# Six more pairs of blocks as seven quarter products, in a hybrid mixer trunk on one Trainium2 core

## The chip, the cores and the metric

The kernel runs as one program on one core of a Trainium2 chip. The time is the device time of one execution in microseconds. Engines are named as in the profile: PE is TensorE, PEld its weight loads, DVE VectorE, ACT ScalarE, POOL GpSimd, SP the sync engine, which issues most DMAs.

## What is computed

The reference is a decoder trunk of one layer: three token mixers side by side, a merge with gates, and a mixture of experts. 512 tokens and 16 meta tokens, width 1024, float32.

```python
u = _rmsnorm(h, norm_mix[layer]) * valid
(a_q, a_f, a_i, a_g, b_qkv, b_beta, b_decay, b_g,
 c_q, c_k, c_v, c_gk, c_g, gate_logits) = jnp.split(u @ w_in[layer], split_points, axis=-1)
y_a = _hgrn2(a_q, a_f, a_i, a_g, ...)                # 4 heads; q = silu(q_in) / sqrt(dk); output * silu(g_in)
y_b = _gated_deltanet(b_qkv, b_beta, b_decay, b_g, ...)   # 4 heads
y_c = _gla(c_q, c_k, c_v, c_gk, c_g, ...)            # 4 heads; output * silu(g_in)
gates = sigmoid(gate_logits)                          # 3 x 1024 columns
merged = sum(gates * (ys @ w_branch))
h = h + merged @ w_out
h = h + _hier_moe(_rmsnorm(h), ...)                   # top 1 of 4 groups, top 2 of 8 experts
```

Everything that this case is about is in `u @ w_in`: blocks of 128 output channels by 512 tokens (528 where the meta tokens are wanted), with 1024 inputs.

## The kernel before

**Stages.** The setup norms and turns the tokens into uT. Then come the first mixer "a" (HGRN2, four heads r = 0 to 3), the second "b" (gated DeltaNet, four heads), the third "c" (GLA, two halves of two heads), the merge, and the experts. "Channel mixer" in the title words of the change is c.

**Blocks and steps.** `blocks` is one list of all blocks of the input projection in the order in which PE computes them and SP loads their weights (512 KB each, into a ring of six). PE interleaves it with the mixers' own products: `fill(n, last)` computes the next n steps of the list (none past block `last`), `through(stage, seg, r)` all steps up to that block. PE's order is thus fixed by hand, and so are those of DVE and ACT, with semaphores counted by name (`Order`). A block of 512 tokens has 8 steps (L822, one product of 512 columns each), a block of 528 ("wide") 8 steps of two products of 264 (L819, L820). Each float32 product is two instructions in the trace.

**Gate pairs.** Two neighbouring blocks of the merge gates ("t0", "t1", and in stage b also "c" t0 to t3) are computed as a pair of seven quarter products, Winograd's form: 14 steps of two products of 256 columns (`pair_step`, L789), 28 products in place of 32 halves. In order P2, P1, P5, P6, P3, P7, P4. It takes four mixes of weights (S1, S2, S4, S3: 128x512 each, on POOL for stage a in `mix_weights`, L672 to L677, on DVE for b and c), four mixes of tokens once (T1 to T4, 128x1024, on POOL), a copy of P1 on ACT (`keep_product`, before P6), and five sums on DVE (`gate_second`: U2, which P7 waits for; `gate_upper`: U3 and upper; `gate_lower`: corner and lower).

**A head of the first mixer.** Blocks f (wide), q, g, v (wide), t0, t1. PE: `a_out(r-1)` (L907, L908, waits for the last pick of head r-1), fill(4), `a_sum(r-1)` (a sum of squares with ones, L901), through g; then `gd` (diagonal Gram product, L848, waits for k and q), fill(3); seven levels l = 0 to 6, each with a Gram product `gr` (it waits for DVE's zb of that level), small products (turn of keys at 0, of values at 2, states at 4) and a fill of 3 steps (2 at levels 5 and 6); then through the next head's f (in head 3, through b's k). DVE per level: d, za, zb, and a pick P (L1467) of the Gram product before. At a head's start ACT and DVE work from f: softplus, log decay, scan b, `a_finish(r-1)` (y1, y: the normed output of the head before), last differences, d0, then q, qe, ke.

**From the first to the second mixer.** After `a_out(3)`, head 0 of b goes fill(3), `a_sum(3)`, through b's q, fill(6), the key's sum of squares `ssk` (L901, four instructions), through v, fill(4), KK (L875), through g, the turn of b_u (`N`, L869), the turn of the keys, and fills of 4. The bank of b's v waits for the convolution of k (`k3`), the bank of b's g for that of q (`q3`). DVE here goes: last pick of head 3 (L1467), gate sums and gate part of the pair (L1564 to L1572), convolution of k (L1696, L1699), `a_finish(3)`, silu and features of k, convolution of q (L1696, L1699), decays, kn, kb, ..., U (b_u, which N waits for).

**The third mixer.** Blocks k, q, g0, g1, v0, v1, then the merge's blocks. PE: fill(4), sum, through q, fill(3), Gram, fill(5), levels with fill(8). DVE copies g0 and g1 out of PSUM at levels 0 and 1.

Of the kernel before, what the change touches and what calls it, by code (L numbers as in the profile page):

```python
# [11 lines left out]
P = 128  # L12
# [92 lines left out]
def hybrid_trunk(nc, x, meta_tokens, norm_mix, w_in, hgrn_lb_logits, hgrn_norm, gdn_conv, gdn_a_log,  # L105
# [4 lines left out]
    with ctx:  # L110
# [272 lines left out]
        A_SEGS = ["f", "q", "g", "v", "t0", "t1"]  # L383
# [3 lines left out]
        blocks = [("a", s, r) for r in range(A_R) for s in A_SEGS]  # L387
# [9 lines left out]
        PAIRS = len(gate_pairs)  # L397

        def pair_no(stage, r):
            return gate_pairs.index((stage, r))  # L400

        def pair_row(stage, r):

            return {"a": 0, "b": KD, "c": 2 * KD}[stage] + 2 * r

        def pair_block(stage, r):

            return where["c", f"t{2 * (r % 2)}", r // 2] if stage == "c" else where[stage, "t0", r]
# [4 lines left out]
        R_AT = {"a": 0, "b": 2, "c": 0}  # L413
        N_AT = {"a": 2, "b": 1, "c": 2}

        def running(stage):

            return bank(R_AT[stage])[:, 0:TH]

        def upper_parts(stage):  # L420

            return ps[:, R_AT[stage] * 512 + TH:R_AT[stage] * 512 + 3 * TH]

        def lower_parts(stage):

            return bank(N_AT[stage])

        def gate_rows(stage, r):
            return gates[:, pair_row(stage, r):pair_row(stage, r) + 2, :]
# [5 lines left out]
        def block_columns(stage, seg, r):  # L435

            if seg[0] == "t":
# [7 lines left out]
        AT = {"a": {"f": wide(0), "q": real(1), "g": real(0), "v": wide(1)},  # L445
              "b": {"k": wide(0), "q": wide(1), "v": wide(0), "g": real(1)},
              "c": {"k": wide(0), "q": real(0), "g0": real(1), "g1": real(0), "v0": wide(1), "v1": wide(0)}}
# [21 lines left out]
        def each(r, names):  # L469
# [8 lines left out]
                                                                               "kv", "gr5", "gr6"])] + each(A_R - 1, ["o", "ss"]))  # L478
        a_act = Order("a_act", [x for r in range(A_R) for x in
                                each(r, ["ab", "e", "l"]) + each(r - 1, ["oo"] if r else []) + each(r, ["ad", "e2", "l2", "k"]) +  # L480
                                each(r - 1, ["ln", "ri"] if r else []) +
                                each(r, ["eb", "dec", "abq", "eq", "lq", "eke", "sq", "xa0", "xb0", "abg", "eg", "lg", "xa1", "xb1",
                                         "sg", "keTm", "keTr", "xa2", "xb2", "vc", "xa3", "xb3", "v", "vm", "xa4", "xb4",
                                         "xa5", "xb5", "xa6", "xb6"])] + each(A_R - 1, ["oo", "ln", "ri"]))
        a_dve = Order("a_dve", [x for r in range(A_R) for x in
                                each(r, ["ls", "dif", "mx", "tk", "lf", "b"]) + each(r - 1, ["y1", "y"] if r else []) +
                                each(r, ["dbm", "dbr", "d0", "tq", "q", "qe", "ke", "d1", "za0", "zb0", "tg", "Pd", "d2", "za1", "zb1",
                                         "g", "P0", "d3", "za2", "zb2", "P1", "d4", "za3", "zb3", "P2", "d5", "za4", "zb4", "P3",
                                         "d6", "za5", "zb5", "S0", "S1", "S2", "S3", "P4", "za6", "zb6", "P5", "P6"])] +
# [40 lines left out]
        def c_finish_names():  # L530
# [8 lines left out]
                                       {0: ["gc_0"], 1: ["gc_1"], 2: ["tg_0"], 3: ["tg_1", "g_0"], 4: ["g_1"], 5: ["S0", "S1", "S2", "S3"]}.get(l, []))] + both([f"P{LEVELS - 1}"]))] +  # L539
                      each(C_R - 1, c_finish_names()))  # L540

        pair_mix = Order("pair_weights", [f"{n}.{p}" for p in range(A_R) for n in ("S1", "S2", "S4", "S3")])
        delta_mix = Order("delta_weights", [f"{n}.{p}" for p in range(A_R, PAIRS) for n in ("S1", "S2", "S4", "S3")])

        def mixed(name, p):
            return (pair_mix if p < A_R else delta_mix).after(f"{name}.{p}")
        pair_pe = Order("pair_products", [f"{n}.{p}" for p in range(PAIRS) for n in ("P1", "P5", "P6", "P3")])
        pair_copy = Order("pair_copies", [f"{n}.{p}" for p in range(PAIRS) for n in ("P1",)])
# [7 lines left out]
        w = Area(WORK)  # L556
        a_fb, a_k, a_b, a_lf, a_tmp, a_eke = (w.take(TOK) for _ in range(6))
        a_q, a_eb, a_qe = (w.take(SEQ) for _ in range(3))
        a_g = w.take(SEQ)
        a_db = w.take(TOK)  # L560
        a_sg = w.take(SEQ)
        a_dd = [w.take(SEQ) for _ in range(2)]
# [2265 lines left out]
```

## Time and profile before

| | us |
|---|---|
| median of 3 runs | 1070.38 |
| runs | 1070.01, 1070.38, 1071.59 |
| profiled execution, its own time | 1071.85 |
| its span, first to last instruction | 1070.0 |
| PE busy | 1027.7 (96%) |
| DVE busy | 533.1 (50%) |
| ACT busy | 309.8 (29%) |
| POOL busy | 93.0 (9%) |

Mean granted clock of PE 0.986. Stage a runs from 17 to about 225 us, b to about 530, c and the merge to about 730, the rest is output product, router and experts. A span's engines overlap, so the shares don't add up; idle time of an engine costs only where PE, or at the end a DMA, has to wait for it. In the timelines, an instruction's duration includes the time in which it overlaps the next of its engine: the cost of one in a run is the distance from start to start.

### The profile page before, as it was taken

The numbers are of one execution on the slowest core, as the hardware profiler recorded it, in microseconds if no ns is written. First come the engines' busy times: TensorE is split into PE (matmuls) and PEld (weight loads), VectorE is DVE, ScalarE is ACT, GpSimd is POOL, SyncE is SP. The second block draws the span as 40 slices with busy tenths as digits, with TensorE's granted clock in tenths as the row PEclk, the third lists the DMA queues.
The fourth block names the chain that finished last, engine by engine and source line by source line (L and its number), as shares of the span: only waits on it lengthen the run. The fifth ranks groups of instructions, "written<-read, shape, count | busy, mean of one in ns | idle before, by whom it ended". The sixth has DMA issues, their size and how long they took to land. (4 is left out here: it accounts for less than half of the span.)

```text
span 1070.0 us, 20467 instructions
## 1 busy us (share of the span) xinstructions
PE 1027.7 (96%) x8841; PEld 696.1 (65%) x8841; DVE 533.1 (50%) x1058; ACT 309.8 (29%) x573; POOL 93.0 (9%) x89
## 2 busy tenths in 40 slices
PE   9999999999999999999999999999998999877897
PEld 8676766787777877878756656544456665545454
DVE  5766566658468477387454365331344322211114
ACT  3545445334243343344332032010110111101013
POOL 4320202000000000000000000000001222112110
PEclk9999999999999999999999999999998999989899
DMA  9222222142332132141222221174947999999986
GB/s 266 66 70 59 60 61 71 49 83 61 80 76 69 41 84 61 42 92 52 59 61 60 59 60 61 40 274 130 386 147 268 415 413 414 416 415 415 417 327 246
DMA packets 111965, 174.73 MB, mean 163 GB/s; under 512 B 9011, under 2 KB 87100, under 8 KB 103554
## 3 DMA queue, kind: packets, MB, share of 16 engines
q1 hardware_dynamic: 99010, 134.93, 36.5%
q10 hardware_dynamic: 7136, 27.33, 6.4%
q0 software_dynamic: 5728, 11.14, 3.9%
q8 instruction: 71, 1.16, 0.4%
q14 instruction: 20, 0.16, 0.0%
HBM read 169.16 MB, written 12.60 MB: 170 GB/s over the span
## 5 line engine op out<-in xcount | busy, mean ns | idle before, releaser
L789 PE MATMUL ps<-arena 128*128 128x256 f32 x672 | 165.0, 388 | 0.0
L789 PEld LDWEIGHTS ps<-arena 128*128 128x128 f32 x672 | 121.2, 190 | 16.4
L822 PE MATMUL ps<-arena 128*128 128x512 f32 x288 | 128.2, 595 | 1.2 <-DVE arena L1831 1.2
L819 PE MATMUL ps<-arena 128*128 128x264 f32 x400 | 123.1, 389 | 0.8 <-DVE gates L1580 0.8
L820 PE MATMUL ps<-arena 128*128 128x264 f32 x400 | 121.7, 386 | 0.0
L2316 PE MATMUL ps<-arena,gates 128*64 128x256 f32 (+1 forms) x1088 | 106.2, 353 | 16.1 <-DMA arena<-in_expert_w_up 15.8
L1463 DVE TENSOR_TENSOR arena<-arena 128x256 f32<-128x256 f32 (+6 forms) x198 | 95.9, 527 | 48.6 <-ACT arena L1259 36.9
L2316 PEld LDWEIGHTS ps<-arena,gates 128*64 128x64 f32 x1088 | 73.6, 145 | 55.7 <-DMA arena<-in_expert_w_up 25.9
L822 PEld LDWEIGHTS ps<-arena 128*128 128x128 f32 x288 | 53.6, 190 | 62.3 <-issue 61.8
L813 PE MATMUL ps<-yT,arena 128*128 128x512 f32 x192 | 84.8, 596 | 2.1 <-DVE gates L1580 1.4
L820 PEld LDWEIGHTS ps<-arena 128*128 128x128 f32 x400 | 76.0, 190 | 13.0
L819 PEld LDWEIGHTS ps<-arena 128*128 128x128 f32 x400 | 72.5, 190 | 13.2 <-issue 2.8
L2495 DVE COPY gates<-ps 128x1024 f32<-128x1024 f32 x15 | 18.4, 1225 | 101.2 <-PE ps L2297 101.1
L813 PEld LDWEIGHTS ps<-yT,arena 128*128 128x128 f32 x192 | 35.7, 190 | 45.0 <-issue 44.6
L1996 PE MATMUL ps<-arena,gates 128*128 128x512 f32 x128 | 55.8, 592 | 0.0
L2252 POOL DMA_INDIRECT gates<-normed_tokens,gates x16 | 16.6, 1036 | 419.4 <-DVE gates L2087 348.5
L2404 ACT ACTIVATE gates<-ps 128x128 f32<-128x128 f32 x32 | 8.9, 278 | 143.9 <-PE ps L2316 143.9
L1996 PEld LDWEIGHTS ps<-arena,gates 128*128 128x128 f32 x128 | 24.0, 190 | 28.7 <-issue 28.2
L2258 POOL DMA_INDIRECT expert_results<-gates x32 | 32.0, 999 | 121.3 <-ACT gates L2410 118.8
L2325 PE MATMUL ps<-arena,gates 128*64 128x512 f32 x176 | 42.3, 604 | 0.0
L2500 DVE TENSOR_TENSOR gates<-gates,ps 128x128 f32<-128x128 f32 x32 | 9.1, 284 | 61.9 <-ACT gates L2404 61.8
L1467 DVE COPY_PREDICATED arena<-C,ps 128x512 f32<-128x512 int32 x56 | 39.8, 724 | 0.0
(374 smaller groups left out, 1372.2 us busy)
## 6 DMA issues: line engine op xcount, KB each, us to landing
arena<-in_w_in SPq DMA_DIRECT2D x68, 512.0 KB, 3.9
arena<-in_expert_w_gate SPq DMA_DIRECT2D x27, 1024.0 KB
arena<-in_expert_w_up SPq DMA_DIRECT2D x27, 1024.0 KB
arena<-in_expert_w_down ACTq DMA_DIRECT2D x16, 1024.0 KB, 33.1
arena<-in_w_branch SPq DMA_DIRECT2D x12, 512.0 KB, 3.9
arena<-in_expert_w_down SPq DMA_DIRECT2D x6, 1024.0 KB, 27.4
C<-in_expert_w_gate SPq DMA_DIRECT2D x5, 1024.0 KB
gates<-in_expert_w_up SPq DMA_DIRECT2D x5, 1024.0 KB
```

The source lines that it names most:

```text
L789: mm = t.matmul(dst, wt[:, k, :], rhs[:, k, :], start=(k == 0), stop=(k == KH - 1))
L813: mm = t.matmul(merge_bank[b], wt, rhs, start=first, stop=last)
L819: t.matmul(dst[:, 0:HALF], wt, uT[:, k, 0:HALF], start=(k == 0), stop=(k == KD - 1))
L820: mm = t.matmul(dst[:, HALF:], wt, uT[:, k, HALF:], start=(k == 0), stop=(k == KD - 1))
L822: mm = t.matmul(dst, wt, uT[:, k, META:], start=(k == 0), stop=(k == KD - 1))
L1463: v.tensor_tensor(out_, a_, b2, op).then_inc(*q.did(name))
L1467: v.copy_predicated(tiles(pm), over(up(l).bitcast(I32), NT), tiles(src)).then_inc(*q.did(name))
L1996: mm = t.matmul(bank(n), gates[:, k, i * P:(i + 1) * P], wo[:, k, n % 2 * 512:(n % 2 + 1) * 512], start=(k == 0), stop=(k == KD - 1))
L2258: return g.indirect_dma_start(out=y_dram, out_offset=bass.IndirectOffsetOnAxis(ap=which, axis=0), in_=rows, in_offset=None, bounds_check=4 ...
L2316: mm = t.matmul(dst, toks[:, k, :], src, start=(k == 0), stop=(k == KD - 1))
L2325: mm = t.matmul(bank(6 + b)[half * SLOTS:(half + 1) * SLOTS, :], hT[b][:, j * SLOTS:(j + 1) * SLOTS], weights[n][1][:, at:at + 512], start ...
L2495: v.tensor_copy(xT[q % 2], ps[:, 0:2 * 512].rearrange("p (k t) -> p k t", k=KD)).then_inc(pair_read.sem, 1)
```

## The change

The query and output gate blocks of each head of a (q, g), and the two output gate blocks of each half of c (g0, g1), become pairs as the gate pairs are: pairs "qg" (running products in PSUM bank 2, lower ones in bank 7 for head 0; banks 0 and 2 for the others) and "g". 18 pairs instead of 12, by `pairs`. Their results go to a_ql and a_gl (two buffers), or c_g, in SBUF. For this:

- The order of blocks in a becomes f, q, g of head 0, then for each head t0, t1, v, and q, g, f of the next head.
- PE goes through t1 before gd, and fills four steps a level (three at level 0), capped at the next head's f, in head 3 at b's q.
- POOL mixes the weights of ten pairs (qg, a and g) instead of four; the token mixes move to DVE, ahead of its first step of the mixers.
- DVE gets five sums for each new pair: a pair's second and upper sums now sit ahead of the levels, its lower ones at level 0, those of the next head's qg at levels 4, 5 and 6. The query of head r+1 is finished (`a_query`: tq, q on DVE, softplus and exponential on ACT) at the end of head r. `gate_end(r)` on ACT moves from head r+1 into head r, behind it.
- In c, two copies on DVE go, the sums of the new pair come at levels 0 and 1, and the fill at level 0 is 6 instead of 8.

The b loop of PE, DVE and ACT isn't changed.

```diff
-        A_SEGS = ["f", "q", "g", "v", "t0", "t1"]
-        blocks = [("a", s, r) for r in range(A_R) for s in A_SEGS]
+        blocks = [("a", s, 0) for s in ("f", "q", "g")]
+        for r in range(A_R):
+            blocks += [("a", s, r) for s in ("t0", "t1", "v")] + [("a", s, r + 1) for s in ("q", "g", "f") if r + 1 < A_R]
...
+        pairs = [("qg", 0)]
+        for r in range(A_R):
+            pairs += [("a", r)] + [("qg", r + 1)] * (r + 1 < A_R)
+        pairs += gate_pairs[A_R:] + [("g", r) for r in range(C_R)]
...
+        def running_bank(stage, r):
+            return {"qg": 0 if r else 2, "a": 2, "b": 2, "c": 0, "g": 2}[stage]
+
+        def lower_bank(stage, r):
+            return {"qg": 2 if r else 7, "a": 0, "b": 1, "c": 2, "g": 0}[stage]
...
             for r in range(A_R - 1):
-                mix_weights(r)
+                mix_weights("qg", r)
+                mix_weights("a", r)
+            mix_weights("qg", A_R - 1)
             g.wait_ge(*dve0.after("gbrow"))
...
+            for r in range(C_R):
+                mix_weights("g", r)
...
             def wait_for_bank(stage, seg, r):
                 if stage == "a":
                     if seg == "f":
+                        pair_upper_free(pair_no("qg", r))
+                    else:
+                        pair_upper_free(pair_no("a", r))
+                elif stage == "b":
+                    if seg == "k":
                         if r:
+                            pair_upper_free(pair_no("c", r - 1))
                         else:
+                            t.wait_ge(*pair_sum.after(f"lower.{pair_no('a', A_R - 1)}"))
                     elif seg == "q":
+                        t.wait_ge(*(pair_sum.after(f"lower.{pair_no('c', r - 1)}") if r else a_act.after(f"vc.{A_R - 1}")))
                     else:
                         t.wait_ge(*b_dve.after(f"{ {'v': 'k3', 'g': 'q3'}[seg]}.{r}"))
...
-            through("a", "q", 0)
+            through("a", "g", 0)
             small_turned()
             for r in range(A_R):
                 if r:
                     a_out(r - 1)
                     fill(4)
                     a_sum(r - 1)
-                through("a", "g", r)
+                through("a", "t1", r)
...
-                    fill(3 if l < 5 else 2)
+                    fill(4 if l else 3, where["a", "f", r + 1] if r + 1 < A_R else where["b", "q", 0])
                 through(*(("a", "f", r + 1) if r + 1 < A_R else ("b", "k", 0)))
...
                     block_grams(c_zz[l % 2], l, r)
-                    fill(8)
+                    fill(8 if l else 6)
...
+            mix_tokens()
             v.wait_ge(sem("consts_loaded"), 16)
...
                 if r:
                     a_finish(r - 1)
+                    second_sum("a", r)
+                else:
+                    second_sum("qg", 0)
                 v.wait_ge(*a_dve.after(f"b.{r}"))
                 last_diffs(a_dve, a_db, a_b, r)
                 diff(a_dve, a_act, a_dd, a_b, 0, r)
...
                 tt(a_dve, f"ke.{r}", a_eke[:, 0:TOK - P], a_eke[:, 0:TOK - P], a_k[:, 0:TOK - P])
+                if r == 0:
+                    second_sum("a", 0)
+                upper_sums("a", r)
...
-                gate_lower("a", r)
                 gate_part("a", r)
+                if r + 1 < A_R:
+                    v.wait_ge(*a_dve.after(f"zb{LEVELS - 1}.{r}"))
+                    a_query(r + 1)
...
+                    if l == 1:
+                        upper_sums("g", r)
                     if l:
                         for s in range(CH):
...
                             pick(c_dve, f"P{l - 1}_{s}.{r}", c_pm[s], l - 1, gram_bank(s))
-                    if l in (0, 1):
-                        v.wait_ge(*block_done("c", f"g{l}", r))
-                        v.tensor_copy(c_g[l], real(1 - l)).then_inc(*c_dve.did(f"gc_{l}.{r}"))
+                    if l == 0:
+                        second_sum("g", r)
+                    if l == 1:
+                        lower_sums("g", r)
```

## Rows read from the trace of the kernel before

**Rows 1.** page of the profile, section 1, busy us of each engine

```profile
PE 1027.7 (96%) x8841; PEld 696.1 (65%) x8841; DVE 533.1 (50%) x1058; ACT 309.8 (29%) x573; POOL 93.0 (9%) x89
```

**Rows 2.** windows: us, busy us of each engine, granted clock, DMA share, GB/s

```profile
77.00:127.00 50.00, 50.00 (x409) 35.85 (x409) 29.82 (x64) 23.87 (x48) 5.28 (x4) 1.00 0.24 64
226.00:252.00 26.00, 26.00 (x115) 19.09 (x114) 19.93 (x31) 12.60 (x19) 1.77 (x2) 1.00 0.43 86
```

**Rows 3.** timeline of TensorE: start us, us, engine, line, operation, tiles, count

```profile
75.14 0.38 PE L907 MATMUL ps<-arena 128*128 128x128 f32 x2
...
81.22 10.46 PE L822 MATMUL ps<-arena 128*128 128x512 f32 x24
91.52 0.29 PE L969 MATMUL ps<-bcol,C 128*128 128x20 f32 x2
...
251.89 3.62 PE L789 MATMUL ps<-arena 128*128 128x256 f32 x16
255.35 0.83 PE L837 MATMUL ps<-arena 128*128 128x128 f32 x6
```

**Rows 4.** page of the profile, section 5, two groups: busy us, mean ns

```profile
L789 PE MATMUL ps<-arena 128*128 128x256 f32 x672 | 165.0, 388 | 0.0
...
L822 PE MATMUL ps<-arena 128*128 128x512 f32 x288 | 128.2, 595 | 1.2 <-DVE arena L1831 1.2
```

**Rows 5.** timeline of the weight loads, head 3 of the first mixer

```profile
205.70 2.46 PEld L789 LDWEIGHTS ps<-arena 128*128 128x128 f32 x12
```

**Rows 6.** timeline of TensorE, head 3 to the second mixer

```profile
191.61 0.46 PE L848 MATMUL ps<-arena 128*32 128x32 f32 x32
...
215.29 0.68 PE L857 MATMUL ps<-arena 128*64 128x64 f32 x8
...
224.85 0.38 PE L907 MATMUL ps<-arena 128*128 128x128 f32 x2
...
226.63 0.61 PE L819 MATMUL ps<-arena 128*128 128x264 f32 x2
...
230.16 0.61 PE L819 MATMUL ps<-arena 128*128 128x264 f32 x2
...
239.96 1.24 PE L901 MATMUL ps<-arena,ones 128*128 128x512 f32 x4
...
250.80 1.25 PE L869 MATMUL ps<-C,arena 128*128 128x128 f32 x10
```

**Rows 7.** timeline of VectorE, the same stretch

```profile
216.53 0.73 DVE L1467 COPY_PREDICATED arena<-C,ps 128x512 f32<-128x512 int32 x1
...
222.35 1.23 DVE L1572 SCALAR_TENSOR_TENSOR gates<-gates,yT 128x1024 f32<-128x1024 f32 x1 [3.40 <-ACT yT L1205]
225.05 0.77 DVE L1696 TENSOR_SCALAR arena<-ps,rowsT 128x528 f32<-128x528 f32 x1 [1.47 <-PE ps L820]
225.85 2.36 DVE L1699 SCALAR_TENSOR_TENSOR arena<-ps,rowsT,arena 128x527 f32<-128x527 f32 x3
...
232.54 0.69 DVE L1463 TENSOR_TENSOR yT<-arena 128x512 f32<-128x512 f32 x1
...
238.37 2.37 DVE L1699 SCALAR_TENSOR_TENSOR arena<-ps,rowsT,arena 128x527 f32<-128x527 f32 x3
...
248.61 0.82 DVE L1463 TENSOR_TENSOR arena<-ps,arena 128x640 f32<-128x640 f32 x1
```

**Rows 8.** windows around an idle stretch in the experts

```profile
810.00:813.40 3.40, 0.12 (x2) 0.04 (x1) 0.00 (x0) 0.00 (x0) 0.00 (x0) 0.82 0.85 339
813.40:819.00 5.60, 5.51 (x42) 5.14 (x44) 3.46 (x7) 0.00 (x0) 0.99 (x1) 0.50 0.15 37
```

**Rows 9.** timeline of VectorE at the start, beside GpSimd

```profile
21.71 2.22 DVE L302 TENSOR_SCALAR lbc<-lbc 128x4 f32<-128x4 f32 x1
```

**Rows 10.** timeline of GpSimd at the start

```profile
21.54 2.36 POOL L659 TENSOR_TENSOR arena<-arena 128x1024 f32<-128x1024 f32 x1
```

**Rows 11.** timeline of VectorE in head 1, last differences

```profile
84.20 1.24 DVE L1463 TENSOR_TENSOR arena<-arena 128x16 f32<-128x16 f32 x3
```

More of the change, by code:

```diff
@@ new lines, in running, with upper_parts, lower_parts, pair_rows @@
+        def running(stage, r):
+            return bank(running_bank(stage, r))[:, 0:TH]
+        def upper_parts(stage, r):
+            at = running_bank(stage, r) * 512 + TH
+            return ps[:, at:at + 2 * TH]
+        def lower_parts(stage, r):
+            return bank(lower_bank(stage, r))
+        def gate_rows(stage, r):
+            row = {"a": 0, "b": KD, "c": 2 * KD}[stage] + 2 * r
+            return gates[:, row:row + 2, :]
+        def pair_rows(stage, r):
+            if stage == "qg":
+                return a_ql, a_gl[r % 2]
+            if stage == "g":
+                return c_g
+            rows = gate_rows(stage, r)
+            return rows[:, 0, :], rows[:, 1, :]
@@ L558, in hybrid_trunk @@
         a_q, a_eb, a_qe = (w.take(SEQ) for _ in range(3))
-        a_g = w.take(SEQ)
+        a_ql = w.take(SEQ)
+        a_gl = [w.take(SEQ) for _ in range(2)]
         a_db = w.take(TOK)
@@ L758, in pair_step @@
                         t.wait_ge(sem(f"block_loaded{n % RING}"), (n // RING + 1) * 16)
+                        if stage == "g":
+                            t.wait_ge(*c_dve.after(f"f.{r}"))
+                        elif stage == "a":
+                            t.wait_ge(*pair_sum.after(f"{'lower' if r else 'upper'}.{p - 1}"))
+                        elif stage == "qg" and r:
+                            t.wait_ge(*pair_sum.after(f"lower.{p - 1}"))
                     if name == "P5":
@@ L1423, in gate_parts @@
                 def gate_parts(s):
[L1424 removed]
+                    a.wait_ge(*pair_sum.after(f"lower.{pair_no('g', r)}"))
                     softplus(c_act, (f"abg_{s}", f"eg_{s}", f"lg_{s}"), r, c_sg[s], c_g[s])
@@ L1568, in gate_part @@
+                v.tensor_tensor(tiles(row, 2), tiles(lower_parts(stage, r), 2), over(row[:, TH:], 2), ALU.add).then_inc(*pair_sum.did(f"lower.{p}"))
             def gate_part(stage, r):
-                p, rows = pair_no(stage, r), gate_rows(stage, r)
+                p, rows = gate_no(stage, r), gate_rows(stage, r)
                 v.wait_ge(*pair_soft.after(f"soft.{p}"))
```

303 lines of the change are left out of this document (164 added, 139 removed).

## The prediction

> **What bounds the kernel now.** I read the page's busy times first. TensorE is busy 96% of the span, VectorE 50%, ScalarE 29%, GpSimd 9% [rows 1]. Then I read the windows of the mixer stages: in the stretches quoted, TensorE is busy for every microsecond, at the full clock (granted 1.00, so 2.4 GHz), while VectorE has 20 us free of 50 in the first mixer and 6 of 26 at the start of the second [rows 2]. So the time of the mixers is the sum of TensorE's instructions. A product removed is time gained, and a microsecond in which TensorE finds nothing ready is a microsecond lost: no later slack takes it back, since the weights of the experts are loaded only when the mixers are done.
>
> **What the seven products save.** Six pairs of blocks change form (four of the first mixer, two of the channel mixer). One of the blocks costs 8 products of 512 columns, recorded as 16 instructions. In an unbroken run of 24 of them the next start comes 10.30 us later, 0.429 us each, so two blocks are 32 x 0.429 = 13.7 us. The new form is 28 products of 256 columns, 56 instructions; 16 of them take 3.46 us to the next start, 0.216 each, so 12.1 us [rows 3]. Saved: 1.63 us a pair, 9.8 us for six. The bound from below is the page's groups: 165.0 us for 672 instructions at L789 is 13.75 us a pair, and 128.2 for 288 at L822 is 14.24, which leaves 0.5 us a pair, 2.9 in all [rows 4]. That mean is not taken: it holds the breaks where other work comes in between, and the number of breaks stays. So 9.8, or 2.9 at worst.
>
> A rule that speaks against this part is a page's. Twelve weight loads of the pair form last 2.46 us in all, less than 12 x 0.216 = 2.59 us of products beside them [rows 3, 5], so the loads lie beside the products. The Trainium skill, TensorE: Matmul & The Clock Gate, section The mechanism, says that a weight load overlaps products in flight only when it goes to another group of rows. If that held here, each load would stand in the row, and the trace disagrees.
>
> **What moves, and what it uncovers: the handover from the first to the second mixer.** This is the largest term. Before, the steps of head 3 that lie between its first Gram product (gd, L848) and the output (a_out) are: v (8 steps), the gate pair (14 steps), b's k (8 steps). Now the gate pair stands before gd, in all heads. In heads 0 to 2 its place in the levels is taken by the next head's query pair and f block. In head 3 there is no next head: the fills are 3, 3, 4, 4, 4, 4, 4, 4 steps, capped at b's q block, and only v, k, q = 24 steps exist. So 2 remain after Gram 5 and none after Gram 6. From gd of head 3 to the turn of b_u (L869) TensorE needed 250.80 - 191.61 = 59.2 us, all busy [rows 6]. It now has one pair less to do there, 12.1 us. The question is whether VectorE and ScalarE can be that much earlier. I follow their chain. Let X be the end of the last pick of head 3, before 217.25 [rows 7].
> 1. Gram 6 ends about 215.97, the pick at 217.25: 1.3 us with nothing to fill, where two steps and the k block were.
> 2. a_out takes 1.8 us (224.85 to 226.63), so it ends at X+1.9. The next fill(3) is now v, whose bank waits for b's k convolution. VectorE is in order: gate part 1.23, convolution 3.16 (225.05 to 228.21): X+4.4. Idle 2.5.
> 3. Three v steps (2.7) and the sum of squares (0.85) end at X+7.95. The normed y of head 3 ends 3.07 us after that product, as before (230.16 to 233.23): X+11.0. TensorE does the five other v steps up to X+12.4.
> 4. fill(6) used to be six v steps. Five are left, so the sixth is the first step of b's output gate, whose bank waits for b's q convolution. That ends 7.5 us after y (240.74 to 233.23), and its order on VectorE is the same: X+18.5. Idle 6.1. The key's sum of squares (L901 x4) stands behind this step in TensorE's queue and waits with it, though its own input is long there.
> 5. Gate step 0.86 and sum of squares (L901 x4) 1.24, end at X+20.6. b_u ends 8.2 us after the latter (241.20 to 249.43): X+28.85. TensorE's work in between is 7.1 us. Idle 1.3.
> Sum 1.3 + 2.5 + 6.1 + 1.3 = 11.2 us [rows 6, 7]. A second way: 24 wide steps and the small products take 29.6 us from gd to X (before 25.6, with 20 steps of which 12 are short, and two after), and 29.0 from X gives 58.6 for 47.1 us of work, 11.5 idle. Bounds 9 to 13.
>
> **The clock.** An idle stretch of 3.3 us is followed by 5.6 us at a granted clock of 0.50, which is 1.2 GHz [rows 8]. The 6.1 us idle of step 4 is longer. Behind it stand a gate step and the sum of squares, on the chain: some 1.9 us of work that takes 3.8. The 2.5 us idle may do it too, with up to 1.7. I take 2.3, bounds 0 and 5. VectorE then runs up to 1.3 us closer to TensorE than before in the rest of b's head 0 (before, b_u was ready 1.4 us early): knock-on waits 0.8, bounds 0 and 1.5.
>
> **Heads 1 and 2: GpSimd beside VectorE.** GpSimd mixes 10 pairs instead of 4; the four token mixes go to VectorE. One of them has 1024 columns, as the gate part has, 1.23 us [rows 7], so 4.9 us for four; the small setup steps around them are stretched no more by GpSimd's mixes of 2.36, and TensorE has f, the small columns and two products to do before the first product that needs them. Hidden, 0 to 1 us. While GpSimd reads SBUF a VectorE operation with SBUF inputs waits: one of 4 elements took 2.22 us beside GpSimd's 2.36 [rows 9, 10]. [...] The mixes for the next query pair come due right after the gate pair's third, fourth and fifth product, which is when VectorE runs y, the last differences, qe and ke of heads 1 and 2. From the end of f (75.14) VectorE has done the differences at 10.3 us [rows 3, 11]. Prices go by the number of columns: 1.23 us for 1024 and 0.69 for 512 [rows 7], so about 0.4 for 256. The chain now starts some 0.7 us later (ScalarE has the query's exponential and the gate's last one, a step of 1024, ahead of it), and gains 0.4 for the second sum, 1.2 for qe and ke, 1.1 for the two upper sums: 13.7. TensorE wants the bank for v at 1.8 + 12.1 + 0.85 + 0.4 = 15.2. Three GpSimd operations of 1.27 us in between would make 17.5, 2.3 late; one or none makes no wait. I take 1.5 a head for two heads, 3.0, bounds 0 and 5. Head 3 has no mix at that place.
>
> **The channel mixer.** For each half VectorE loses two copies and gains five sums. At level 1 the upper sums wait for the sixth product of the pair, and the two picks of level 0 queue behind them on VectorE: 1.1 + 2 x 0.8 = 2.7 us from that product's end, where TensorE has only the seventh product and the key turn left before Gram 1, 1.73 + 0.4. So Gram 1 waits 0.6 us in each half, 1.2, bounds 0 and 2.5 (none before, when nothing stood ahead of the picks). GpSimd's mixes for the first of them fall into the end of the second mixer: 0 to 1, taken as 0 since VectorE reads PSUM there.
>
> Otherwise the five new sums of a pair (3 x 0.4 + 2 x 0.69 = 2.6 us) and ScalarE's copy are hidden: VectorE is busy 29.8 us of the 50 of a head [rows 2], and a fill is now four steps, 3.46 us, where it was three. Without that cover they would cost 4 x 2.6 = 10 us.
>
> **Sum.** -9.8 + 11.2 + 2.3 + 0.8 + 3.0 + 1.2 = +8.7 us. The profiled execution took 1071.85 us (span 1070.0 and 1.85 around it), 1.5 above the median of 1070.38, and just over the slowest run shown; the difference applies to either. From the median: 1079.1; from the profiled one 1080.6.
>
> **The rivals.**
> - Faster: the handover is covered after all. Its mechanism: the chain from gd of head 3 to b_u is paced by TensorE alone, and shortens with it by 12 us. It decides at the wait of b's first gate step for the q convolution: if that is under 2 us, the saving wins. Then 1070.4 - 9.8 + 1 to 3 = 1060.6 to 1064, say 1062. For it speaks that VectorE has 6 us of 26 free in that stretch [rows 2]; against it that the steps of the chain wait for each other, not for TensorE. Chance 0.11.
> - Nothing to be seen: the handover costs as reckoned, without clock, GpSimd and channel terms, or about half of all: -9.8 + 9 to 11: 1070 to 1072. Chance 0.10.
> - Slower by more: the saving is the page's mean (2.9), or each GpSimd mix blocks VectorE in the levels as well: +15.6 or more, 1086 to 1090. Chance 0.07.
> - Weight loads stand in the row with the products. One lasts 0.205 us [rows 5]. A pair would then pay 24 loads more, 4.9 us, less the 1.6: +3.3 a pair, +19.8 us for six in place of -9.8, so 1079.1 + 29.6 = 1108.7. The rows show the loads beside the products in this very form. The Trainium skill's page on TensorE, named above, is where this rule stands. Chance 0.01.
>
> **How the numbers follow.** The forecast, slower through the handover, 1073 to 1086, has 0.71. Range 1066 to 1087: the lower end leaves out the faster rival, the upper one most of the two slower ones. About 0.2% (2.1 us) is what a measurement here can tell from no change. Faster by more than that 0.11 (the first rival), within it 0.10 (the second), slower 0.79 (the rest).
>
> **What would show it.** Right: in the waits of TensorE a new row of about 6 us for the first b gate step (L822's successor) on VectorE's convolution, one of 2.5 us for b's v block on the same line, a granted clock below 1 in that window alone of the mixers; heads of the first mixer 1.6 us shorter each, but for what GpSimd costs in heads 1 and 2 (a wait of v for the upper sums); 0.6 us at the channel mixer's Gram 1. Wrong: no idle above 2 us between the mixers, or new records of L789 clearly over 0.216 us apart within a run.

## The result and the profile after

The changed kernel takes 1079.3 us (median of 4 runs, 1076.9 to 1080.6), where the kernel before took 1070.6 beside it. The ratio is 1.0078, with a 95% interval of 1.0058 to 1.0097: slower, by 0.6 to 1.0%. The profiled execution took 1079.32 us, its span 1077.5.

The page's busy times, which answer to [rows 1]:

```profile
PE 1021.9 (95%) x8985; PEld 723.8 (67%) x8985; DVE 552.3 (51%) x1088; ACT 310.4 (29%) x579; POOL 113.5 (11%) x109
```

TensorE is busy 5.8 us less than before and its span is 7.5 us longer. The products were saved; idle time grew. The waits of TensorE say where (line waited for: us in total, times, longest). The rows of the mixers that before did not have:

```profile
PE ps L853 <- DVE arena L1783: 6.1, 1, 6.1
...
PE ps L850 <- DVE arena L1783: 2.2, 1, 2.2
PE ps L850 <- DVE gates L1620: 2.2, 2, 1.2
...
PE ps L1129 <- DVE arena L1514: 1.1, 2, 0.5
...
PE ps L938 <- DVE arena L1514: 0.9, 1, 0.9
...
PE ps L920 <- DVE arena L1510: 0.6, 1, 0.6
PE ps L900 <- DVE arena L1510: 0.6, 1, 0.6
```

Line numbers have moved: L853 is the product of 512 columns (before L822), L820 the quarter product (L789), L850 and L851 the wide block (L819, L820), L879 gd (L848), L892 the Gram products of the levels (L861), L1129 those of the channel mixer (L1098), L932 the sums of squares (L901), L900 the turn (L869), L920 small products of the second mixer (L889), L938 a_out (L907), L1783 the convolutions on VectorE (L1699), L1510 its differences, products and turns (L1463), L1514 its picks (L1467), L1620 the upper sums.

The timeline of TensorE from the last Gram product of head 3 to the turn of b_u, which answers to [rows 6]:

```profile
199.39 0.46 PE L879 MATMUL ps<-arena 128*32 128x32 f32 x32
...
228.50 0.49 PE L938 MATMUL ps<-arena 128*128 128x128 f32 x2 [0.88 <-DVE arena L1514]
...
232.78 0.68 PE L850 MATMUL ps<-arena 128*128 128x264 f32 x2 [2.22 <-DVE arena L1783]
...
235.52 1.02 PE L932 MATMUL ps<-arena,ones 128*128 128x512 f32 x2
...
247.07 2.04 PE L853 MATMUL ps<-arena 128*128 128x512 f32 x2 [6.07 <-DVE arena L1783]
248.90 2.34 PE L932 MATMUL ps<-arena,ones 128*128 128x512 f32 x4
251.04 4.24 PE L853 MATMUL ps<-arena 128*128 128x512 f32 x8
...
259.53 1.31 PE L900 MATMUL ps<-C,arena 128*128 128x128 f32 x10 [0.56 <-DVE arena L1510]
```

The squares that the second L932 (of four instructions) waits for are done on ScalarE before that:

```profile
243.88 0.74 ACT L1402 ACTIVATE arena<-arena 128x640 f32<-128x640 f32 x1 [0.84 <-DVE arena L1510]
```

Before, the same stretch of 59.2 us had no idle time; now it is 60.1 us with four idles, 9.73 in all, though one pair of blocks (12.1 us) has left it. The windows of the stretch, of the idle and of what follows (us, busy us of each engine, granted clock, DMA share, GB/s):

```profile
199.40:259.50 60.10, 50.40 (x410) 36.62 (x409) 36.65 (x72) 21.74 (x40) 1.76 (x2) 0.94 0.29 63
240.90:247.10 6.20, 0.13 (x2) 0.06 (x1) 5.10 (x9) 2.10 (x3) 0.60 (x1) 0.87 0.85 111
247.10:252.30 5.20, 5.20 (x8) 2.55 (x9) 1.28 (x2) 0.99 (x2) 0.00 (x0) 0.50 0.48 98
```

While TensorE stands idle, VectorE is busy 5.10 us of 6.20: the chain is there. The granted clock falls to 0.50 before the idle ends (0.87 is its mean over the second window), and the 5.2 us behind the idle run at it.

The stages, from the start times of the same instructions in the timelines (us, from one profiled execution of each kernel; N is the turn of b_u in head 0 of the second mixer, L900 x10, c the first forget product of the third mixer, w the first output product behind the merge; differences are taken before rounding):

| | gd of heads 0, 1, 2, 3 | N | c | w | end |
|---|---|---|---|---|---|
| before | 41.9, 92.0, 141.9, 191.6 | 250.8 | 531.0 | 728.8 | 1070.0 |
| after | 52.3, 100.7, 150.1, 199.4 | 259.5 | 539.8 | 735.5 | 1077.5 |
| difference | +10.4, +8.8, +8.2, +7.8 | +8.7 | +8.8 | +6.6 | +7.5 |

The +10.4 at gd of head 0 is no loss: the pair a of that head (12.1) now stands ahead of it, less the saving of the query pair (1.63). It leaves +6.6 us at w. The last 0.9 behind it can't be put down to the change: from w to the end it took 341.2 us before and 340.6 to 346.4 in the kernels below, whose code is the same there. TensorE waits there for expert weights 21 to 28 us in all, another amount in each execution. These waits alone don't explain the scatter (the stage of 346.4 us, in e3, has only 22.0 us of them), and its cause stays open. In after the two rows are

```profile
PE ps L2403 <- DMA arena<-in_expert_w_up: 15.8, 7, 3.4
PE ps L2403 <- DMA gates<-in_expert_w_up: 6.7, 3, 3.2
```

The totals of one kernel scatter by 2 to 7 us, while c to w repeats to 0.1 us wherever nothing in it differs. N to c repeats less well: 278.7 to 281.8 us, though the code in it hardly differs. That is why the experiments are read in stages as well as in totals.

### The profile page after: what moved, and what is told of

Same layout as the page of the kernel before. It is cut to its first block, busy times and chain, and to the rows that moved or that the text cites. A ratio compares the mean times of both kernels' runs of the same rounds, so it can differ in the third digit from the quotient of the medians.

```text
span 1077.5 us, 20878 instructions
## 1 busy us (share of the span) xinstructions
PE 1021.9 (95%) x8985; PEld 723.8 (67%) x8985; DVE 552.3 (51%) x1088; ACT 310.4 (29%) x579; POOL 113.5 (11%) x109
## 4 chain that ended last, share of the span: by engine, by line
PE 74%; DMA 14%; DVE 6%; ACT 2%; SPq 2%; issue 2%; POOL 0%; DVEq 0%; POOLq 0%; ACTq 0%
PE ps L820 18%; PE ps L850 8%; PE ps L844 8%; DMA gates<-in_expert_w_up 8%; PE ps L851 8%; PE ps L2403 6%; DMA arena<-in_expert_w_up 4%; PE ps L853 3%; PE ps L2083 3%; PE ps L2412 2%; PE ps L920 2%; DVE arena L1510 2%; PE ps L932 1%; DMA arena<-expert_results 1%; PE ps L1093 1%
## 5 line engine op out<-in xcount | busy, mean ns | idle before, releaser
L820 PE MATMUL ps<-arena 128*128 128x256 f32 x1008 | 237.7, 385 | 0.0
L820 PEld LDWEIGHTS ps<-arena 128*128 128x128 f32 x1008 | 185.1, 190 | 27.5 <-issue 3.1
L1510 DVE TENSOR_TENSOR arena<-arena 128x256 f32<-128x256 f32 (+6 forms) x202 | 110.6, 588 | 54.5 <-ACT arena L1302 37.0
L850 PE MATMUL ps<-arena 128*128 128x264 f32 x400 | 123.9, 392 | 5.2 <-DVE arena L1783 2.2
L851 PE MATMUL ps<-arena 128*128 128x264 f32 x400 | 121.7, 386 | 0.0
L2403 PEld LDWEIGHTS ps<-arena,gates 128*64 128x64 f32 x1088 | 72.7, 143 | 55.4 <-DMA arena<-in_expert_w_up 25.5
L851 PEld LDWEIGHTS ps<-arena 128*128 128x128 f32 x400 | 76.0, 190 | 13.0
L850 PEld LDWEIGHTS ps<-arena 128*128 128x128 f32 x400 | 71.8, 190 | 17.8 <-issue 7.6
L853 PE MATMUL ps<-arena 128*128 128x512 f32 x96 | 45.1, 611 | 7.3 <-DVE arena L1783 6.1
L1514 DVE COPY_PREDICATED arena<-C,ps 128x512 f32<-128x512 int32 x56 | 39.7, 721 | 0.0
L2497 ACT ACTIVATE gates<-ps 128x512 f32<-128x512 f32 x32 | 19.1, 597 | 70.6 <-PE ps L2412 70.6
```

What stands on the lines that cost most here:

```text
L820: mm = t.matmul(dst, wt[:, k, :], rhs[:, k, :], start=(k == 0), stop=(k == KH - 1))
L850: t.matmul(dst[:, 0:HALF], wt, uT[:, k, 0:HALF], start=(k == 0), stop=(k == KD - 1))
L851: mm = t.matmul(dst[:, HALF:], wt, uT[:, k, HALF:], start=(k == 0), stop=(k == KD - 1))
L853: mm = t.matmul(dst, wt, uT[:, k, META:], start=(k == 0), stop=(k == KD - 1))
L1510: v.tensor_tensor(out_, a_, b2, op).then_inc(*q.did(name))
L1514: v.copy_predicated(tiles(pm), over(up(l).bitcast(I32), NT), tiles(src)).then_inc(*q.did(name))
```

## The experiments

All kernels were timed beside the kernel before, whose medians were 1071.8, 1072.3 and 1072.0 us in the three comparisons; the ratios are to that one. The first comparison holds e1 to e4, the second e5 to e8, the third e9 to e11; after and before are from the section above. Each median is of 4 to 12 runs, but that of e7 of 2; each stage is from one profiled execution.

| kernel | median us | ratio to before, 95% | gd 3 to N | gd 0 to w | c to w |
|---|---|---|---|---|---|
| before | 1070.6 | | 59.2 | 686.9 | 197.8 |
| after | 1079.3 | 1.0078 (1.0058 to 1.0097) | 60.1 | 683.1 | 195.7 |
| e1, third mixer alone | 1072.7 | 0.9997 (0.9983 to 1.0011) | 59.2 | 685.5 | 195.7 |
| e2, first mixer alone | 1079.6 | 1.0067 (1.0050 to 1.0084) | 61.9 | 686.6 | 197.8 |
| e3, needless products | 1079.7 | 1.0076 (1.0060 to 1.0092) | 58.2 | 682.7 | 195.7 |
| e4, query convolved early | 1074.8 | 1.0031 (1.0019 to 1.0043) | 56.9 | 679.8 | 195.7 |
| e5, fills of three | 1069.3 | 0.9972 (0.9961 to 0.9983) | 50.6 | 672.9 | 195.7 |
| e6, mixes later | 1080.8 | 1.0083 (1.0066 to 1.0101) | 61.8 | 685.8 | 195.7 |
| e7, picks first | 1078.0 | 1.0052 (1.0034 to 1.0069) | 60.2 | 682.0 | 194.5 |
| e8, all four | 1068.1 | 0.9959 (0.9946 to 0.9972) | 51.8 | 673.1 | 194.5 |
| e9, gate step behind the sum | 1074.8 | 1.0023 (1.0010 to 1.0036) | 58.5 | 680.0 | 195.7 |
| e10, nine steps | 1066.8 | 0.9949 (0.9929 to 0.9968) | 51.4 | 671.8 | 194.5 |
| e11, query in its place | 1067.9 | 0.9963 (0.9950 to 0.9976) | 53.2 | 672.6 | 194.5 |

(For "gd 0 to w", before and e1 have 10.4 us more in it than the others for the reason above: compare them as 676.5 and 675.1.)

**e1, the channel mixer's pairs alone.** The kernel before with

```diff
+        pairs = gate_pairs + [("g", r) for r in range(C_R)]
...
-              "c": {"k": wide(0), "q": real(0), "g0": real(1), "g1": real(0), "v0": wide(1), "v1": wide(0)}}
+              "c": {"k": wide(0), "q": real(0), "v0": wide(1), "v1": wide(0)}}
```

and the products, sums and mixes that belong to it.

> The kernel before, with nothing of the change but the channel mixer's two output gates (g0, g1) as pairs of seven quarter products. My theory: each of the two pairs saves 1.63 us of TensorE, 3.3 together, and the first Gram product of each half waits for the pick by what the new kernel showed there, 0.54 and 0.53. So 2.2 us faster than before, 1068.4, and these two idles in the trace. Rival, each term of the change is as large as the whole is slower: the quarter products are dearer in the stage than in an unbroken run (the page's means, 0.5 us a pair): then 0, 1070.6. Slower than before by more than 1 would say that the sums on VectorE cost more than the idles show.

The stage from c to w falls from 197.8 to 195.7, the expected 2.2 to a tenth, and Gram 1 waits as it does in after:

```profile
PE ps L1120 <- DVE arena L1492: 1.1, 2, 0.5
```

So 3.2 us are saved and 1.1 given back. The total doesn't show it: 0.9997, and 2.2 us (0.9979) lie just outside the interval. The profiled execution had 0.8 us more between N and c (281.0 against 280.2): two idles for which the profile names no releaser, 1.23 and 0.68 us, were 0.71 and 0.42 before. The part is worth what was expected in its stage; that the whole kernel gains it is not shown by this run.

**e2, the first mixer's pairs alone.** The kernel after with g0 and g1 as real blocks again:

```diff
-        pairs += gate_pairs[A_R:] + [("g", r) for r in range(C_R)]
+        pairs += gate_pairs[A_R:]
```

> The kernel after, with the channel mixer's two gates put back as real blocks, so only the first mixer's pairs are left. My theory: the loss is all in the first mixer and the handover, so this is 2.2 us slower than the kernel after: 1081.5, 10.9 over before. The turn of the second mixer's first head is 8.7 us later than before, as in the kernel after, and the start of the channel mixer too. Rival, the channel mixer takes part in the loss: 1079.3 or less.

1079.6, and not 1081.5: by its total alone this kernel can't be told from after, which is what the rival said. The stages decide. From c to w it takes the 197.8 us of before, while its gd stand as far apart as in after (48.4, 49.4, 49.3 us) and its handover has the same idles (0.88, 2.22, 6.09, 0.37). So the whole loss is in the first mixer and the handover; the 2.1 us of the channel mixer are in the stage and not in the total. gd 3 to N is 61.9 and not 60.1, and the windows say why: the idle of 2.22 us was followed by a low clock too in this execution (the same in e6, 61.8; not in after, e3, e4, e7 and e9, which have that idle too).

```profile
232.70:236.10 3.40, 3.40 (x9) 2.63 (x9) 0.00 (x0) 0.00 (x0) 0.00 (x0) 0.50 0.00 0
```

**e3, needless work in the idle.**

```diff
-                fill(6)
+                if r == 0:
+                    fill(5)
+                    for _ in range(14):
+                        t.matmul(bank(5)[:, 0:TH], ones[:, :], uT[:, 0, META:META + TH], start=True, stop=True)
+                    fill(1)
+                else:
+                    fill(6)
```

> The kernel after with 14 needless products of 256 columns added (28 records, 28 x 0.216 = 6.05 us of TensorE's work, into a bank that nobody reads), just ahead of the first output-gate step of the second mixer's head 0, where TensorE stood idle for 6.07 us. My theory: the stretch is set by the chain on VectorE, so this work costs nothing; and as TensorE no longer stands idle its clock stays at 1.00 where it was 0.50 for 6.8 us, which gives 1.9 to 2.6 us back: 1076.7 to 1077.4, faster than the kernel after though it computes more. Rival one, time is the sum of TensorE's instructions here as well: 6 us more, 1085. Rival two, the chain sets it but the low clock cost nothing, as the work behind it had slack: 1079.3.

Six microseconds of added work on an engine that is 95% busy cost nothing: 1079.7. The windows of the stretch and of the two parts that were idle and slow in after:

```profile
198.50:256.60 58.10, 54.10 (x438) 40.73 (x437) 36.65 (x72) 21.79 (x40) 1.76 (x2) 1.00 0.30 65
240.00:246.00 6.00, 6.00 (x29) 5.06 (x27) 5.02 (x8) 2.11 (x3) 0.60 (x1) 1.00 0.81 94
246.00:252.30 6.30, 6.23 (x19) 2.91 (x19) 3.55 (x6) 3.84 (x6) 0.00 (x0) 1.00 0.42 97
```

The stretch is 2.0 us shorter than in after and the clock is 1.00 throughout. So the sum-of-instructions rival falls for this stretch: the chain sets it. The clock's price is 2.0 us there. The total doesn't show it (ratios 1.0076 and 1.0078, where 1076.7 to 1077.4 us had been expected): in the profiled execution 1.5 us went again between N and c (281.8 against 280.3). Half of that are idles: two of 0.68 and 0.41 us at 421 and 430 us, for which the profile names no releaser, are there as they are before, and not in after. The rest of it I can't place.

```profile
421.65 0.32 PE L920 MATMUL ps<-arena 64*32 64x32 f32 x12 [0.68 <-issue]
```

**e4, the query convolved behind the key** on VectorE, in head 0 of b:

```diff
                 convolve("k", ck, wide(0), r)
+                if r == 0:
+                    convolve("q", cq, wide(1), r)
...
                 unit("k", b_kf, ck, b_em, r)
-                convolve("q", cq, wide(1), r)
+                if r:
+                    convolve("q", cq, wide(1), r)
```

> The kernel after with one move on VectorE, in the second mixer's head 0: its query is convolved straight behind its key, before the last head of the first mixer is finished. My theory: the idle of 6.07 us before the first output-gate step was the wait for that convolution. It ends 9 us earlier now, so the gate step waits for nothing; what is late next is the sum of the key's squares, whose input on ScalarE needs the key's convolution and which the finish of head 3 precedes: an idle of about 3 us in place of 6, the clock low for less time or not at all, 4.3 us faster than after: 1075. Rival, the idle is set by another chain and the convolution is just the last named: the idle stays within 1 us of 6.07 and the time at 1079.

1074.8, as expected, and the waits name the next one in line:

```profile
PE ps L932 <- ACT arena L1402: 2.8, 1, 2.8
```

**e5, the steps dealt out thinly** in head 3 of the first mixer:

```diff
-                    fill(4 if l else 3, where["a", "f", r + 1] if r + 1 < A_R else where["b", "q", 0])
+                    if r + 1 < A_R:
+                        fill(4 if l else 3, where["a", "f", r + 1])
+                    else:
+                        fill(3 if l < 5 else 2, where["b", "q", 0])
```

> The kernel after, with the steps of the last head of the first mixer dealt out more thinly: 3, 3, 3, 3, 3, 3, 2, 2 where they were 3, 3, 4, 4, 4, 4, and then 2 and 0. The same instructions, in another place. My theory: TensorE has two steps (1.7 us) beside the last pick, where it waited 0.88, and two fewer v steps wait behind the key's convolution, where it waited 2.22: both idles go or fall under 0.5 us, the 6.07 before the first gate step stays, so from the last head's first Gram product to the first turn of the second mixer it takes 57 us in place of 60.1, and the whole 1076.3. Rival: the steps are as many, and the idle time just moves to the levels above, where the picks are then not covered: 60.1 us for the stretch and the time of the kernel after.

The edit brought three times what was expected (57 and 1076.3): 50.6 us for the stretch and 1069.3 for the whole, faster than the kernel before. All that is left of the idles:

```profile
239.33 1.35 PE L932 MATMUL ps<-arena,ones 128*128 128x512 f32 x4 [2.79 <-ACT arena L1405]
241.73 3.67 PE L853 MATMUL ps<-arena 128*128 128x512 f32 x8 [0.16 <-DVE arena L1786]
```

The first line is the key's sum of squares, and it now stands *ahead* of the first gate step. That is what I had overlooked. With the steps dealt out thinly, 22 of the 24 are used up at the last level and 2 are left for behind a_out; fill(3) then takes only one v step and fill(6) finds seven v steps. In after all 24 were gone before the last pick: fill(3) took three of b's eight v steps, fill(6) found five and took a gate step, and that one waited for the query's convolution with the key's sum behind it. So the gain is 0.88 + 2.22, and 3.28 of the 6.07, 0.40 for the rest, and the clock's 2.6: 9.4 of the 9.6 measured.

**e9, that step alone.** One number of the kernel after:

```diff
-                fill(6)
+                fill(6 if r else 5)
```

> The kernel after with one number changed: in the second mixer's head 0 five steps stand ahead of the sum of the key's squares and not six, so that the first output-gate step stands behind that sum in TensorE's queue and not ahead of it. My theory, after the fills of three: most of the 6.07 us is the price of this one step in the wrong place, since the squares are ready 2.4 us before the query's convolution (244.62 against 247.06 in the kernel after). Now the sum waits about 3.6 us and the gate step 1.2 behind it, so the key's chain starts 3.3 us earlier: from the last head's first Gram product to the first turn 56 to 57 us where it took 60.1, the whole about 1075.5, and the two idles of 0.88 and 2.22 ahead of it stay. Rival: the convolution of the query paces the chain anyway, 60 us and 1079.

1074.8, and the two waits are near those forecast, 3.6 and 1.2 (timeline; behind it the window of what follows):

```profile
244.96 1.43 PE L932 MATMUL ps<-arena,ones 128*128 128x512 f32 x4 [3.68 <-ACT arena L1402]
247.37 5.46 PE L853 MATMUL ps<-arena 128*128 128x512 f32 x6 [0.97 <-DVE arena L1783]
```

```profile
246.10:252.90 6.80, 5.83 (x9) 2.48 (x9) 5.48 (x9) 4.71 (x7) 0.00 (x0) 0.50 0.50 127
```

The stretch is 58.5 and not 56 to 57. The window is why: the clock is low for 5.83 us of work here, 2.9 us lost, since this edit takes none of the idle of 3.68 away; I had left the clock out. The turn waits for nothing, so TensorE's own slowed work is what ends last; 58.5 less 2.9 is 55.6. Behind N this kernel takes 1.5 us less than after (c − N is 278.8 against 280.3), 0.9 of it by the small idles that after has there.

**e6, GpSimd's mixes held back** for heads 1 to 3:

```diff
+                if stage == "qg" and r:
+                    g.wait_ge(*pair_sum.after(f"upper.{p - 1}"))
```

> The kernel after with GpSimd's mixes for the query pairs of heads 1 to 3 held back until the upper sums of the gate pair before them are done. Theory: the waits of 1.05 and 1.17 us of the v block in heads 1 and 2 come from GpSimd's two operations beside VectorE's five (5.23 us together, some 2.45 alone): without that neighbour both waits go, the distance between the first Gram products of heads 1 and 2, and of 2 and 3, falls from 49.4 and 49.3 to the 48.4 of the undisturbed one, and the whole is 2.2 us shorter, 1077.1. Rival: VectorE is late from the chain before (the exponential of the query and the gate), and GpSimd only runs at that time: the waits stay at 1 us. A second risk: the query pair now waits for its mixes, seen as a wait for GpSimd.

In after, head 2 shows what the mixes do, beside head 3, which has none (the five operations of VectorE are the last differences, d0, qe and ke, all with both inputs in SBUF; L694 and L695 are GpSimd's mixes):

```profile
144.92 1.27 POOL L690 TENSOR_TENSOR arena<-arena 128x512 f32<-128x512 f32 x1 [0.42 <-POOL arena L685]
...
145.30 5.23 DVE L1510 TENSOR_TENSOR arena<-arena 128x16 f32<-128x16 f32 x5
146.65 1.77 POOL L694 TENSOR_TENSOR arena<-arena 128x512 f32<-128x512 f32 x1 [0.47 <-PE ps L820]
...
148.38 1.72 POOL L695 TENSOR_TENSOR arena<-arena 128x512 f32<-128x512 f32 x1
...
151.74 0.68 PE L850 MATMUL ps<-arena 128*128 128x264 f32 x2 [1.17 <-DVE gates L1620]
...
194.66 2.48 DVE L1510 TENSOR_TENSOR arena<-arena 128x16 f32<-128x16 f32 x5
```

5.23 us beside GpSimd, 2.48 without. The Trainium skill, SBUF — State Buffer, section Who interferes with whom, calls this an exclusive lock of a shared port pair; these rows agree as far as the sizes go: the excess of 2.75 us is less than GpSimd's 1.77 + 1.72, so it can be time spent waiting for them, but the rows don't show who held what.

Both waits of v went with the mixes moved, so the neighbour was their cause. But the collision moved with them, to the first level. In head 0, which had no wait before, three of VectorE's operations took 3.50 us beside GpSimd's mixes (the first row is the same three in after), and Gram 0 and 1 wait, 1.16 and 0.81 us; in heads 1 and 2 Gram 0 now waits 0.39 and 0.69:

```profile
52.60 1.36 DVE L1510 TENSOR_TENSOR arena<-arena 128x512 f32<-128x512 f32 x3
...
52.96 3.50 DVE L1512 TENSOR_TENSOR arena<-arena 128x512 f32<-128x512 f32 x3
53.08 1.69 POOL L692 TENSOR_TENSOR arena<-arena 128x512 f32<-128x512 f32 x1
```

```profile
PE ps L894 <- DVE arena L1512: 3.1, 4, 1.2
```

The distances between the gd are 50.5, 48.8 and 48.8, where after has 48.4, 49.4 and 49.3: 2.1 lost, 1.1 won. A third outcome, neither the theory's nor the rival's. What follows is to hold them back in heads 1 and 2 alone, as e10 and e11 do: 48.4, 48.8 and 48.8 in e10. The 1080.8 us of the whole also hold a second stretch of low clock, behind the idle of 2.22 us (gd 3 to N is 61.8).

**e7, the picks ahead of the upper sums** at level 1 of the channel mixer.

```diff
-                    if l == 1:
-                        upper_sums("g", r)
...
                     if l == 1:
+                        upper_sums("g", r)
                         lower_sums("g", r)
```

> The kernel after with the channel mixer's upper sums of a gate pair put behind the two picks of level 0 on VectorE instead of ahead of them. Theory: the 0.54 and 0.53 us that the first Gram product of each half waits are the time of these sums; both go, and the stretch from the channel mixer's first forget product to its output's first product falls from 195.7 to 194.6 us. The whole, 1.1 us less, is too little to be seen. Rival: the picks are late because of their own input, and nothing moves: 195.7.

195.7 falls to 194.5 and both waits of L1129 are gone.

**e8, e10, e11, combinations.** e8 is e4 to e7 together. e10 is e8 with `if stage == "qg" and r > 1` and `fill(6 if r else 9)`. e11 is e10 without the early convolution, with fill(6).

> The kernel after with the four edits together: the query convolved behind the key, the steps dealt out 3, 3, 3, 3, 3, 3, 2, 2, GpSimd's mixes held back, and the picks ahead of the sums. My theory says that the losses are separate idles and their gains add: 4.5 (measured) + 3.1 + 2.2 + 1.1 from the kernel after's 1079.3, 1068.4, and since the saving of the products (9.8) is real, faster than the kernel before, by 2 to 4 us. From the last head's first Gram product to the first turn 53 to 54 us, where it took 59.2 before. Rival: what is taken from one idle turns up in the next, as one chain paces them all (the idle of 2.8 us that was left with the query convolved early grows): then 1073 to 1075, no faster than before.

> The four edits together, with two differences: GpSimd's mixes are held back in heads 1 and 2 alone (holding them back in head 0 lengthened it by 2.2 us), and nine steps instead of six stand ahead of the sum of the key's squares, two of them output-gate steps whose bank is free early here. Theory: the last idle of the handover, 2.79 us, is filled with work that has to be done anyway, since behind that sum TensorE paced the stretch: from the last head's first Gram product to the first turn 48.5 to 49.5 us (51.8 with six), head 0 back to 48.4, so 2 + 2.5 us under the 1068.1 of the four edits: 1063.6. Rival: the chain on VectorE and ScalarE paces the turn, the idle only moves to it: 1066.

> The kernel after with the fills of three, the picks ahead of the sums and GpSimd's mixes held back in heads 1 and 2 alone, the query's convolution left where it was. Theory: with the steps dealt out thinly, no output-gate step stands ahead of the key's sum, so the early convolution brings nothing: 50.6 us from the last head's first Gram product to the first turn, as with the fills alone (against 51.8 of the four edits); the mixes give 0.7 + 0.5, the picks 1.1: 1069.3 - 2.3 = 1067.0. Rival, the early convolution was part of the gain: over 1068.

All three are faster than the kernel before, by 0.4 to 0.5%. e8: 1068.1, the number of the theory, but not by its sum: e5 alone had brought 10 us and not 3.1, and e4 adds nothing to it (51.8 and 50.6; in e8 the clock is low for 3.4 us of work there, which is 1.7 us lost, in e5 it is not), since both remove the same wait. e10, for which 1063.6 was expected: the idle ahead of the key's sum is filled (0.20 left), and the time turns up behind it, where TensorE waits for the key (L1838) and for b_u (L1515):

```profile
244.77 1.38 PE L908 MATMUL ps<-arena 128*128 128x128 f32 x10 [1.63 <-DVE arena L1838]
249.60 1.31 PE L902 MATMUL ps<-C,arena 128*128 128x128 f32 x10 [1.74 <-DVE arena L1515]
```

So the rival was right there: from a_out on, the chain on VectorE and ScalarE paces the turn at about 51 us, and filling its gaps with needed work wins little (e10's 1066.8 is not told from e11's 1067.9). e11: 1067.9 against 1067.0 expected; its stretch is 53.2 with 6.8 us of low clock, beginning 0.6 us before the end of the same idle of 2.80 us that left the clock at 1.00 in e5 (the first window; the second is e5's, for its stretch of 50.6 us):

```profile
236.90:243.70 6.80, 6.19 (x11) 3.62 (x12) 6.02 (x9) 4.14 (x7) 0.00 (x0) 0.51 0.43 88
...
199.20:249.80 50.60, 47.64 (x411) 35.49 (x411) 36.88 (x73) 21.79 (x40) 1.77 (x2) 1.00 0.34 75
```

## Why the prediction was right, point by point

**The saving, −9.8: right.** From gd 0 to gd 1, which has no wait of its own (that of 1.05 us comes behind gd 1), the distance fell from 50.06 to 48.42: 1.64 for a pair. In the channel mixer 2.1 + 1.1 of waits is 3.2 for two. The bound of 2.9 in all is out. The page's groups, which answer to [rows 4]:

```profile
L820 PE MATMUL ps<-arena 128*128 128x256 f32 x1008 | 237.7, 385 | 0.0
...
L853 PE MATMUL ps<-arena 128*128 128x512 f32 x96 | 45.1, 611 | 7.3 <-DVE arena L1783 6.1
```

336 instructions more for 72.7 us, 0.216 each, and 192 fewer for 83.1. An unbroken run of the new form, products and loads:

```profile
87.34 3.62 PE L820 MATMUL ps<-arena 128*128 128x256 f32 x16
...
91.66 8.80 PE L820 MATMUL ps<-arena 128*128 128x256 f32 x40
100.29 0.29 PE L1000 MATMUL ps<-bcol,C 128*128 128x20 f32 x2
```

```profile
91.66 8.39 PEld L820 LDWEIGHTS ps<-arena 128*128 128x128 f32 x39 [0.24 <-issue]
```

40 products in 8.63 us, and 39 loads that take 8.39 us beside them. The rival of loads in the row is out, and with it, for this form, the rule of the Trainium skill's page TensorE: Matmul & The Clock Gate, section The mechanism, that a load overlaps only products of other row groups. (The same section also lets a load go ahead when it is for a background weight buffer; no run here tells whether these do.)

**The handover, 11.2: its four waits are where the steps put them,** 1.3, 2.5, 6.1 and 1.3 expected, 0.88, 2.22, 6.07 and 0.56 measured, 9.73 in all. gd 3 to N was to be 58.6 and 2.3 for the clock, 60.9; it is 60.1. The last pick ends at gd + 29.1 and not at 29.6. The last wait is smaller in part because the low clock stretches TensorE's own work ahead of it: in e3, with the clock at 1.00, it is 0.88.

One sentence of step 4 was wrong: that the input of the key's sum "is long there" while it waits behind the gate step. The squares (L1402 on ScalarE, 243.88 + 0.74) end at 244.62 in after, and the gate step starts at 247.07. Of the 6.07 us only 2.4 come from the order of the two; 3.68 stay when it is put right (e9), because a_out is so late that the key's own chain is late. What made it expensive is that the 24 steps left to head 3 were used up too early; dealt out by the old numbers (e5) the same change is a gain. The prediction had counted that the steps run out; that the key's own chain would be late as well, so that under half of the 6.07 us hangs on the order of two steps, it didn't have.

**The clock, 2.3:** 5.20 us of work at 0.50, so 2.6 us; e3 gives 2.0 for the same thing. Right, and so was the doubt on the 2.5 us idle: 1.7 us more in two of seven executions of that idle.

**Knock-on 0.8: too large.** Idles of 0.59 and 0.33 appear behind N, but those of 0.71 and 0.42 that before has later go. N to c takes 280.2 and 280.3: nothing.

**Heads 1 and 2, 3.0:** waits of 1.05 and 1.17 for the upper sums, so 2.2. Mechanism right (e6), size a third too large.

**The channel mixer, 1.2:** 0.54 + 0.53 = 1.07. Right.

With these sizes the sum is −9.8 + 9.7 + 2.6 + 0 + 2.2 + 1.1 = +5.8. The table of stages has +6.6 at w. Of the 0.8 between them, 0.7 stand in gd 3 to N, where TensorE's busy time at full clock is 50.40 − 2.60 = 47.8 against the 47.1 reckoned (e5 has 47.6 there with the clock at 1.00); I have no cause for that. The measured medians differ by 8.7 us, the very sum that was forecast, but part of that agreement is luck: the terms come to 5.8 and the stages up to w to 6.6, at the low end of the interval of the ratio (6.2 to 10.4 us), and what is over that can't be told from the scatter of stages that the change leaves alone.

## What to carry to other kernels

When work is taken out of an interleaved order, count what is left to fill with behind each later wait, and deal it out again: here the products saved 10 us and the handover's idle and clock took 12 back, and dealing one head's fills out by threes instead of fours made the slower kernel a faster one. Look above all for a filler step that itself waits and stands ahead of a step on the chain, since an in-order queue then adds its wait to the chain. To learn whether a stretch is set by the busiest engine or by a chain beside it, put needless work into its idle: here 6 us of it cost nothing.

## What the runs showed of the hardware

- With an idle of 6.1 us on TensorE came 6.8 us at the lower of its two clock levels (granted 0.50) in after, e2, e6 and e7, beginning 1.2 to 2.2 us before the idle ended. With one of 3.68 us came 6.8 us (e9), beginning 1.2 us behind its end; with one of 2.8 us none (e5), 3.4 (e4, e8) or 6.8 us (e11); with one of 2.22 us none (five executions) or 3.4 us (e2, e6). The length of the idle alone doesn't tell which.
- Operations of VectorE with both inputs in SBUF beside GpSimd's: five took 5.23 us against 2.48, and three 3.50 against 1.36; GpSimd's own took 1.77 and 1.72, where another of the same form (144.92) takes 1.27. Both engines pay, and moving one of them only changes which operations meet.
